# Causal attention's VectorE order, and the last two projections and norms by token halves

## The reference

```python
# differential attention, per head of 4: two causal softmaxes, combined with lambda
a = softmax(q1 @ k1.T + bias) - lam * softmax(q2 @ k2.T + bias)      # 128-query tiles
y = rmsnorm(a @ v)
merged = g_a * (y_a @ proj_a) + g_b * (y_b @ proj_b) + g_c * (y_c @ proj_c)
# second block, for each of its two layers
sh, sc, gt = split(silu(c) @ w_ada[i] + b_ada[i], 3)
u = rms_norm(h, norm_g[i]) * (1.0 + sc) + sh
h = h + gt * mixer_i(u)                # mixer 0: latent attention, mixer 1: Fourier
# Fourier mixer
proj = u @ w_in; z, gate = proj[..., :1024], proj[..., 1024:]
y = fftn(z in 8 groups of 128, axes=(token, feature), norm="ortho").real
out = (y * silu(gate)) @ w_out
return rms_norm(h, final_g)
```

## Time and profile before

| | |
|---|---|
| median of 3 runs (lowest, highest) | 2641.75 us (2641.52, 2643.74) |
| the profiled execution: time, span | 2648.13 us, 2646.1 us |
| TensorE busy, mean granted clock | 2532.6 us (96%), 0.982 |
| VectorE, ScalarE, GpSimd busy | 1395.9, 702.4, 676.0 us |
| causal attention, about | 160 to 670 us of the span |
| out2 with norm4 up to the first Fourier transform | 2272 to 2313 us |
| final norm and output | 2624 to 2646 us |

### The profile page before, as it was taken

How to read it: one execution, slowest core, us unless ns; L and a number is a source line. 1 busy time by engine, 2 the same in 40 slices (tenths; PEclk the granted TensorE clock), 3 DMA queues, 4 the chain that set the end, 5 groups by cost and what they waited for, 6 DMA issues and landing times.

```text
span 2646.1 us, 32721 instructions
## 1 busy us (share of the span) xinstructions
PE 2532.6 (96%) x12324; PEld 2087.7 (79%) x12324; DVE 1395.9 (53%) x1780; ACT 702.4 (27%) x993; POOL 676.0 (26%) x368
## 2 busy tenths in 40 slices
PE   7999999999999999999999989999999989899997
PEld 5777777777787888888888868888888878688875
DVE  7856664734644552355135673277777764534344
ACT  4232222222211110011001232065666651222121
POOL 3232322322333333333333422200000003222221
PEclk9999999999999999999999989999999999899998
DMA  4133333422321111111121111100000002111011
GB/s 169 47 115 132 104 128 112 136 80 81 127 87 48 48 48 48 49 53 49 48 64 48 56 45 37 48 17 9 16 8 8 9 9 66 32 32 40 32 40 71
DMA packets 44681, 158.17 MB, mean 60 GB/s; under 512 B 5396, under 2 KB 6676, under 8 KB 44474
## 3 DMA queue, kind: packets, MB, share of 16 engines
q1 hardware_dynamic: 38596, 135.15, 15.5%
q10 hardware_dynamic: 6006, 21.93, 2.3%
HBM read 146.03 MB, written 13.39 MB: 60 GB/s over the span
## 4 chain that ended last, share of the span: by engine, by line
PE 84%; DVE 11%; issue 3%; ACT 1%; DVEq 0%; DMA 0%; ACTq 0%; SPq 0%
PE PS L556 65%; PE PS L1019 4%; PE PS L952 3%; PE PS L958 2%; PE PS L991 2%; DVE SC L1891 1%; PE PS L597 1%; DVE cols L2221 1%; PE PS L589 1%; PE PS L942 1%; PE PS L744 1%; DVE H L1708 1%; PE PS L709 1%; DVE SC L1848 1%; PE PS L1108 1%
## 5 line engine op out<-in xcount | busy, mean ns | idle before, releaser
L556 PE MATMUL PS<-H,w_hl 128*128 128x512 f32 x6624 | 1552.6, 394 | 52.2 <-DVE H L1708 18.4
L556 PEld LDWEIGHTS PS<-H,w_hl 128*128 128x128 f32 x6624 | 1246.5, 189 | 338.5 <-issue 45.3
L531 POOL CAST w_hl<-w_raw 128x1024 fp32r<-128x1024 f32 x180 | 200.4, 1113 | 1906.7 <-PE PS L556 1490.6
L533 POOL TENSOR_TENSOR w_hl<-w_raw,w_hl 128x1024 fp32r<-128x1024 f32 x180 | 466.0, 2589 | 14.4
L556 PE MATMUL PS<-FF,w_hl 128*128 128x512 f32 x1056 | 239.8, 389 | 0.0
L556 PEld LDWEIGHTS PS<-FF,w_hl 128*128 128x128 f32 x1056 | 198.3, 188 | 41.1
L952 PE MATMUL PS<-CKV,QN 128*128 128x512 f32 (+1 forms) x576 | 141.9, 364 | 0.0
L1435 ACT ACTIVATE SC<-SC,vec 128x1024 f32<-128x1024 f32 x22 | 25.4, 1152 | 392.5 <-DVE SC L2087 392.4
L1019 PE MATMUL PS<-PT,CKT 128*128 128x256 f32 x960 | 123.3, 287 | 1.5 <-DVE PT L2237 1.5
L1019 PEld LDWEIGHTS PS<-PT,CKT 128*128 128x128 f32 x960 | 120.3, 195 | 2.4 <-DVE PT L2237 1.7
L2237 DVE TENSOR_TENSOR PT<-PS,PT 128x512 fp32r<-128x512 f32 (+1 forms) x192 | 103.6, 596 | 22.9 <-ACT PT L1531 22.4
(11 more groups left out here) (298 smaller groups left out, 2407.5 us busy)
## 6 DMA issues: line engine op xcount, KB each, us to landing
w_raw<-in_units SPq DMA_DIRECT2D x182, 512.0 KB, 3.5
AW<-in_ada SPq DMA_DIRECT2D x48, 512.0 KB, 4.1
X<-in_x SPq DMA_DIRECT2D x8, 512.0 KB, 9.7
SC<-in_x ACTq DMA_DIRECT2D x8, 512.0 KB, 3.5
out<-X ACTq DMA_DIRECT2D x8, 512.0 KB, 3.1
m_part<-GTA ACTq DMA_DIRECT2D x7, 512.0 KB, 4.0
M<-m_part SPq DMA_DIRECT2D x7, 512.0 KB, 7.3
g_part<-GTB ACTq DMA_DIRECT2D x6, 512.0 KB, 2.8
```

The lines of the kernel that those rows point to most:

```text
L531: pool.tensor_copy(hi_part, raw).then_inc(w_hi, 1)
L533: pool.tensor_tensor(lo_part, raw, hi_part.bitcast(F32), ALU.subtract).then_inc(w_split, 1)
L556: mm = pe.matmul(PS[:, out_at + a:out_at + a + m], w(s, wp, w0 + k), src[:, o:o + m], start=(k == 0 and wp == 0 and xp == 0), stop=(k == k ...
```

## The change

Five things change.

1. In `diff_head` on VectorE, `combine(t + 1)` stands ahead of the copy of OC.
2. `biased(t + 2)` runs the first half of `slot(t, 1)` between its two rows, the second half behind them.
3. `ada_places` puts one tile behind a query tile that weighs pa or pb itself or has such a slot first in the next, else three (two behind the last query tile).
4. out2 and out3: the last two units run by token halves (unit 6 first half, unit 7 first half, unit 6 second half with the sum and, behind it, the spread of the first half's norm, unit 7 second half). Residual, squares, mean, root and diagonal go by halves, and the second half's steps lie between the scaling (norm4) or output (final) steps of the first half. The first Fourier group is taken out of its loop and made by halves too: z first half with the second half's sum in its middle and its spread behind, gate first half, z second half, gate second half up to k < 6.
5. The outputs leave in 16 DMAs of 128x512 from SyncE's queue in place of 8 of 128x1024 from ScalarE's.

The diff, cut (`half_rows`, `half_add`, `half_means`, `half_diagonal`, `half_make`, `half_low` are L2008, L2017, L1670, L1675 with L1685, L1695 and L1708 on 512 tokens):

```diff
-    ("out2", {0: 4, 1: 5, "unit": 8, "xnew": 9, "square": 9}),
-    ("norm4", {**NORM, "split": 8}),
+    ("out2", {0: 5, 1: 5, "unit": 8, "xnew": 10, "square": 10}),
+    ("norm4", {**HALF_NORMS, "split": 16}),
-    ("out3", {0: 4, 1: 5, "unit": 8, "xnew": 9, "square": 9}),
-    ("final", {**NORM}),
+    ("out3", {0: 5, 1: 5, "unit": 8, "xnew": 10, "square": 10}),
+    ("final", {**HALF_NORMS}),
...
+def weighs(h, t, n):
+    return any(kind in ("pa", "pb") for kind, _, _ in SLOTS[h].get((t, n), []))
...
-        weighed = [t for t in range(QT_N) for s in range(2) for kind, _, half in SLOTS[h].get((t, s), [])
-                   if kind == "pb" and half == 0]
-        here = sorted([("out", t) for t in range(QT_N)] + [("out", t) for t in range(QT_N) if t not in weighed],
-                      key=lambda at: at[1])
+        here = []
+        for t in range(QT_N):
+            few = weighs(h, t, 0) or weighs(h, t, 1) or weighs(h, t + 1, 0)
+            here += [("out", t)] * (1 if few else 2 if t + 1 == QT_N else 3)
...
+        for half in range(2):
+            for c in range(KC):
+                part = slice(half * HALF, (half + 1) * HALF)
+                sp.wait_ge(o_ready, half * KC + c + 1)
+                sp.dma_start(out[c][:, part], X[:, c * T + half * HALF:c * T + (half + 1) * HALF]).then_inc(o_out, 16)
+        sp.wait_ge(o_out, 16 * 2 * KC)
...
-        project("out2", 0, H2, KC, before("out2", "split"), halves=True)
-        phase_norm("norm4", early=before("norm4", "square") - 1)
+        def half_sum(phase, half):
+            take(2, b(phase, 2) + half)
+            pe.wait_ge(acc_ready, b(phase, "norm") + half + 1)
+            for j in range(4 * half, 4 * half + 4):
+                mm = pe.matmul(PS[:, 2048 + j:2049 + j], ACC[:, j * P:(j + 1) * P], ones[:, 0:1], start=True, stop=True)
+            mm.then_inc(done[2], 1)
+        def half_spread(phase, half):
+            take(3, b(phase, 3) + half)
+            pe.wait_ge(diag_ready, (b(phase, "norm") + half) * 2 + 2)
+            pe.matmul(PS[:, 3072 + half * HALF:3072 + (half + 1) * HALF], ones[:, :],
+                      DIAG[:, half * HALF:(half + 1) * HALF], start=True, stop=True).then_inc(done[3], 1)
+        def project_by_halves(phase, norm, ready):
...
+            for s in range(2):
+                turn(KC // 2 - 1, s, HALF)
+            feature_major(u0 % 2, H2, KC * T, T, KC, 0, a0=HALF, opens=False, k1=4)
+            half_sum(norm, 0)
+            feature_major(u0 % 2, H2, KC * T, T, KC, 0, a0=HALF, opens=False, k0=4).then_inc(done[0], 1)
+            half_spread(norm, 0)
+            feature_major((u0 + 1) % 2, H2, KC * T, T, KC, 1024, a0=HALF).then_inc(done[1], 1)
...
+        def fourier(i, first=False):
...
-                if s == 0:
-                    feature_major(u0 % 2, H2, KC * T, T, KC, 0, ready=before("norm4", "split")).then_inc(done[0], 1)
+                if first and s == 0:
+                    feature_major(u0 % 2, H2, KC * T, T, KC, 0, n=HALF, ready=split, k1=4)
+                    half_sum("norm4", 1)
+                    feature_major(u0 % 2, H2, KC * T, T, KC, 0, n=HALF, opens=False, ready=split, k0=4)
+                    half_spread("norm4", 1)
+                elif first:
+                    feature_major((u0 + 1) % 2, H2, KC * T, T, KC, 1024, n=HALF, opens=False)
+                    feature_major(u0 % 2, H2, KC * T, T, KC, 0, a0=HALF, opens=False, ready=split + KC
+                                  ).then_inc(done[0], 1)
+                    feature_major((u0 + 1) % 2, H2, KC * T, T, KC, 1024, a0=HALF, k1=6)
...
-            feature_major((u0 + 1) % 2, H2, KC * T, T, KC, 1024, opens=False, k0=6).then_inc(done[1], 1)
+            feature_major((u0 + 1) % 2, H2, KC * T, T, KC, 1024, a0=HALF if first else 0, opens=False, k0=6
...
-        project("out3", 0, H2, KC, before("out3", "split"), halves=True)
-        phase_norm("final", early=before("final", "square") - 1)
+        fourier(0, first=True)
+        with pe.Fori(1, FG) as i:
+            fourier(i)
+        project_by_halves("out3", "final", before("out3", "split") - KC)
+        half_sum("final", 1)
+        half_spread("final", 1)
...
+        last_squares("out2", "norm4")
+        for c in range(KC):
+            half_hi(c, 0)
+            if c == 4:
+                half_square("out2", 1, 1)
+            elif c == 6:
+                half_root("norm4", 1)
+        for c in range(KC):
+            half_hi(c, 1)
...
-        residual("out3")
-        phase_norm("final")
-        for c in range(KC):
-            act.wait_ge(o_ready, c + 1)
-            act.dma_start(out[c], X[:, c * T:(c + 1) * T]).then_inc(o_out, 16)
-        act.wait_ge(o_out, 16 * KC)
+        last_squares("out3", "final")
+        half_square("out3", 1, 1)
+        half_root("final", 1)
...
-        def biased(h, t):
+        def biased(h, t, between=None):
...
+                if c == 0 and between:
+                    between()
...
-        def slot(h, t, n):
+        def slot(h, t, n, halves=(0, 1)):
-                if kind in ("pa", "pb"):
+                if kind in ("pa", "pb") and half in halves:
                     weighted(kind, i, half)
...
         def diff_head(h):
             for t in range(QT_N):
                 slot(h, t, 0)
+                if t + 1 < QT_N:
+                    combine(h, t + 1)
                 v.wait_ge(done[1], before("diff", 1) + 17 * h + 3 + 2 * t)
                 chain(v.tensor_copy(OC[:, t * P:(t + 1) * P], PS[:, 1024:1024 + P]))
                 v.sem_inc(free[1], 1)
                 v.sem_inc(oc_ready, 1)
-                if t + 1 < QT_N:
-                    combine(h, t + 1)
                 if t + 2 < QT_N:
-                    biased(h, t + 2)
-                slot(h, t, 1)
+                    biased(h, t + 2, between=lambda: slot(h, t, 1, (0,)))
+                    slot(h, t, 1, (1,))
+                else:
+                    slot(h, t, 1)
                 ada_at(h, t, "out")
...
-        residual("out2", 0, gain=modl[:, 0:8])
-        phase_scale("norm4", D, 1e-6)
-        apply_split(H2, KC * T, X, KC, T, lambda c: fac1[:, c:c + 1], lambda c: modl[:, 8 + c:9 + c])
...
+            acs[0] += KC - 2
+            for s in range(2):
+                half_rows(phase, gain, s, 0)
+                half_add(s, 0)
+            half_means(norm, 0)
+            half_diagonal(norm, 0)
+            half_rows(phase, gain, 0, 1)
+            half_add(0, 1)
...
+        residual_by_halves("out2", "norm4", modl[:, 0:8])
+        for half in range(2):
+            v.wait_ge(done[3], before("norm4", 3) + half + 1)
+            if half == 0:
+                v.sem_inc(free[3], 1)
+            half_make(0, half)
+            for c in range(KC):
+                if c + 1 < KC:
+                    half_make(c + 1, half)
+                half_low(c, half)
+                if half == 0 and c == 3:
+                    half_rows("out2", modl[:, 0:8], 1, 1)
+                elif half == 0 and c == 4:
+                    half_add(1, 1)
+                elif half == 0 and c == 5:
+                    half_means("norm4", 1)
+                elif half == 0 and c == 6:
+                    half_diagonal("norm4", 1)
+        v.sem_inc(free[3], 1)
...
-        residual("out3", 0, gain=modl[:, 24:32])
-        phase_scale("final", D, 1e-6)
-        for c in range(KC):
-            v.scalar_tensor_tensor(out=x, in0=x, scalar=v1("final_g2", c), in1=PS[:, 3072:4096],
-                                   op0=ALU.mult, op1=ALU.mult).then_inc(o_ready, 1)
+        residual_by_halves("out3", "final", modl[:, 24:32])
+        for half in range(2):
+            if half:
+                half_diagonal("final", 1)
+            v.wait_ge(done[3], before("final", 3) + half + 1)
+            v.sem_inc(free[3], 1)
+            for c in range(KC):
+                x = X[:, c * T + half * HALF:c * T + (half + 1) * HALF]
+                v.scalar_tensor_tensor(out=x, in0=x, scalar=v1("final_g2", c),
+                                       in1=PS[:, 3072 + half * HALF:3072 + (half + 1) * HALF],
+                                       op0=ALU.mult, op1=ALU.mult).then_inc(o_ready, 1)
+                if half == 0 and c == 6:
+                    half_rows("out3", modl[:, 24:32], 1, 1)
+            if half == 0:
+                half_add(1, 1)
+                half_means("final", 1)
```

More of the change, by code:

```diff
@@ new lines, in half_add, with half_means @@
+        def half_add(s, half):
+            sqs[0] += 1
+            acs[0] += 1
+            part = slice(half * HALF, (half + 1) * HALF)
+            v.wait_ge(sq_ready, sqs[0])
+            v.tensor_tensor(ACC[:, part], ACC[:, part], SQ[:, part], ALU.add).then_inc(sq_added, 1)
+            v.wait_ge(sq_added, acs[0])
+            if s:
+                v.sem_inc(acc_ready, 1)
+        def half_means(norm, half):
+            v.wait_ge(done[2], before(norm, 2) + half + 1)
```

(28 more changed lines are left out.)

65 lines of the change are left out of this document (60 added, 5 removed).

## The result

| | before | after |
|---|---|---|
| median | 2642.15 us | 2623.07 us (2619.43 to 2624.79, 4 runs) |
| profiled execution, span | 2646.1 us | 2619.9 us |

The ratio is 0.9925, 95% interval 0.991 to 0.9939: 19.1 us faster, where 40 were forecast, and outside the range of 2594 to 2614.

The account below looks back on a forecast made before the run. TensorE, busy 96% of the span, bounds the kernel; VectorE, idle elsewhere, holds it up by its order. Gains 23.5 + 11.9 + 4.7 = 40.1 off 2641.75 gave about 2602 us, range 2597 to 2609 (8 in 10 with both rivals: 2594 to 2614).

Parts of the forecast that it names:

- Part A: Causal attention: VectorE's new order and ada places take off 23.5 us, bounds 24.3 and 12.
- Hence the 11.3 us go: Causal attention: with the combination ahead of the copy of OC, the transposes' 11.3 us of waits for VectorE go.
- they go too: Causal attention: dense matmuls' waits, 8.3 and 3.1 us, go, the first pb half being weighed one row of scores earlier.
- The 1.6 for the clock: Causal attention: without the 2.66 us wait, 1.6 of 1.8 us lost to the low clock behind it come back.
- one ada tile ahead of a weighing is harmless: Causal attention: waits of 2.89 and 2.66 us behind two ada tiles ahead of a weighing go, where now one stands.
- The three-tile blocks at no cost: Causal attention: VectorE stands about 3 us for each of eight blocks' third tile; cost taken as 0, at most 24.
- Rival 1: Causal attention: the waits come back in other places; price half of Part A, 12 us, time 2614; chance 0.12.
- Part B: From out2's last matmul to the first transform: 40.7 us becomes 28.0, net 11.9 off; bounds 13 and 4.
- a step of scaling or low part costs 0.65: Behind out2 on VectorE: each step takes 0.65 us, so eight chunks, 16 steps, take 10.4 per half.
- 0.7 twice, 1.4: Behind out2: GpSimd's subtraction lengthens a VectorE low part by 0.7 us, twice, 1.4 in all.
- Part C: From out3's last matmul to the end: 22.4 us becomes 15.5, net 4.7 off; bounds 3 and 6.5.
- rival 2: Behind out2: low clock costs 5 us, VectorE stopped for GpSimd's whole splits 3.4; price 8.4, time 2610; chance 0.1.

Follow-up runs that it names:

- short_ada: The changed kernel with every ada product over 128 of its 1024 columns (wrong values): 2612.68 us, ratio 0.9886 to the kernel before.
- after_cast: The changed kernel with GpSimd's subtraction replaced by a second cast (low parts of weights wrong): 2602.67 us, ratio 0.9846 to the kernel before.
- new_places: The changed kernel with no ada tile behind a query tile whose successor weighs first, one behind a weighing tile, three elsewhere: 2613.42 us.

## Why the prediction was wrong

**Bound of the kernel.** TensorE's waits came from VectorE: right. "So it has time enough and is held in the wrong place" is the step that failed: 109.3 us is a sum over tiles, and in tiles that weigh VectorE has none to spare. short_ada, after_cast and new_places each took work or stretching off it there and gave 9 to 10 us in attention, each with 7 to 8 us less of TensorE's standing and without the fall of the clock.

**Part A, 23.5 forecast, 10.1 measured.** TensorE stood 9.7 us less and was busy 0.4 less. "Hence the 11.3 us go" and "they go too" counted two waits as independent that one engine's time stood behind. The waits at the transposes fell by 5.9, but the combination ahead of the copy then delayed halves; undone, the stage was the same. The 1.6 for the clock did not come back: the fall behind the 2.66 us wait in head 1 is gone, and one in head 0 came for it. That one ada tile ahead of a weighing is harmless was the costliest error (9.4, of it some 2 by the clock). The three-tile blocks at no cost: right; the loads stood in VectorE's time 13.4 us and in nobody else's. Rival 1 had this mechanism at 12 us and chance 0.12; it was too low.

**Part B, 11.9 forecast, 4.7 measured.** The order of events was as worked out; 28.0 became 35.2, 7.2 more. By the trace, counted from out2's last matmul:

| step | forecast, us | measured, us | more |
|---|---|---|---|
| first chunk begins | -4.4 | -3.1 | 1.3 |
| first half on VectorE | 14.3 | 16.9 | 2.6 |
| last low part to second half | 2.0 | 3.0 | 1.0 |
| second half on VectorE | 10.4 | 12.0 | 1.6 |
| from there to the transform | 5.7 | 6.4 | 0.7 |

The term that was sized most wrongly is "a step of scaling or low part costs 0.65": a chunk takes 1.45 and not 1.30, in 16 chunks 2.4. The steps put between the chunks of the first half took 3.5 and not 2.5. "0.7 twice, 1.4" for GpSimd's subtraction was nearly right: 1.6, by the two low parts in the trace and the comparison with after_cast. Of the late start 0.8 is a sum of squares that took 1.45 beside GpSimd's cast, where it takes 0.69 by itself; the prediction had no term for that. The 1.0 ahead of the second half is the low clock (of before: the earlier trace rows): from the last low part to the spread it took TensorE 1.6 at 0.50 for three matmuls, and not 0.7. By the lock rule of the Trainium skill (SBUF — State Buffer, "SBUF: two separate sides") two subtractions could have cost all of the 1.4 + 3.4 = 4.8. The steps agree with it almost in full in when they end: the low part from 2261.10 ended 0.55 us behind the subtraction that ended at 2262.63, the ada product from 453.71 ended 1.08 behind that of 455.98, where they take 0.75 and 1.23 by themselves. The price was 1.6 all the same, for beside each subtraction VectorE also made scalings with an operand in PSUM, which kept their 0.75, and only the low part behind them waited for the rest. In attention the prediction had no term for it, and there the stretched product of 3.35 us stood ahead of the longest wait, 2.53 us.

**Part C, 4.7 forecast, 4.3 measured.** Right: last norm row, sum on TensorE, spread and eight scaled halves came in that order, and the eight took 5.35 where 5.2 were forecast.

**Rivals together.** 2602 + 12 + 8 = 2622 is near the measured 2623, and for rival 1 that is its mechanism (12 priced, 13.4 measured). For rival 2 it is luck in good part: 7.2 was missing in its stage, but its own terms, a low clock through the gate's first half (5) and subtractions that stop VectorE for their whole length (3.4), did not come; the clock was back at 1.00 from 2274 and cost about 1.0, the subtractions 0.2 more than forecast. The rest was VectorE's steps. Both shortfalls come from VectorE being fuller than I took it, and they sit in different stages, though the rivals were given as exclusive cases. A slip beside it: 43.8 off is 2598, not the 2597 of the range.

## What to carry to other kernels

Idle time of an engine summed over a stage says nothing about the tile in which others wait for it: lay its queue out over one such tile, with its slowest observed step and not the median. Where a wait is removed by moving work ahead of it, look at what the moved work now stands ahead of. Rivals that touch different stages add up; price them together too. Split what a version gives into the idle and the busy time of the waiting engine: here a part of each of the larger differences was TensorE's clock and not the wait.
